# A recurrence kernel on one core: each power's transpose is squared beside the power instead of being turned from it

## The chip, the core and the metric

The kernel runs on one core of a Trainium2 chip. Its engines are TensorE (PE in the profile, PEld its weight loads), VectorE (DVE), ScalarE (ACT), GpSimd (POOL) and SyncE (SP, which here issues loads and stores). Each engine works through its own instructions in order; an instruction may wait for a semaphore that another engine raises, and what stands behind it on its engine waits too. Matmul results land in PSUM, where ACT and DVE read them. The metric is the time of one execution on the device, in microseconds; less is better.

## What is computed

The reference is one inference step of a two-layer trunk, on 128 context tokens and 512 latent tokens. Layer 0 mixes attention with a gated recurrence in two directions (cut to what matters here):

```
def _rwkv_step(S, xs):
    r, w, k, v, kk, a = xs
    sa = jnp.einsum('bhij,bhj->bhi', S, -kk)
    S = S * w[:, :, None, :] + sa[..., None] * (kk * a)[:, :, None, :] + v[..., None] * k[:, :, None, :]
    return S, jnp.einsum('bhij,bhj->bhi', S, r)
...
yf, sf = direction(wdf, adf, 0, s0f, False)
yb, sb = direction(wdb, adb, 1, s0b, True)
```

A scan over T tokens, forward and backward, for 8 heads with a state of 64x64 each. The rest of the program (attention, a gated feed-forward layer, a second layer with a mixture of experts) is not touched.

## The kernel before

The kernel does not walk token by token. It takes chunks of 128 tokens and, within a chunk, halves of 64 (HALVES, partitions 0 to 63 and 64 to 127). Inside a half the recurrence is a triangular system (I - A) u = rhs, with A strictly triangular, 64x64. Its inverse is the product of I + A^(2^l) for l = 0 to 5, so the kernel squares A five times (LEVELS = 5) and at each level multiplies the running inverse by the new power.

The function rwkv_stage has 20 **steps**: four pairs of heads (ct = 0 to 3) times five chunks (i = 0 to 4). In each step both directions (d = 0, 1), both heads of the pair (hh) and both halves (b) are done. The matrices of a step and where they lie:

- X holds the powers: X[b, slot, d, hh, 1, :] is the power, X[b, slot, d, hh, 0, :] its transpose; the two slots alternate by level. At level 0 the transpose is the masked product AM itself. The profile calls X a_power and AM a_masked.
- pU[d] is two PSUM banks for each direction (p_unit): bank 0 takes squares and turnings, bank 1 the products with the inverse. The inverse is TF (inverse_t).

A matmul takes a left operand that is already transposed, so squaring a power needs both the power and its transpose. Before the change a level goes like this, on PE and ACT by turns:

1. square_pe (L2318): four 64x64 products for each direction.
2. square_act (L2451): ACT copies the four results from PSUM to X as the new power.
3. power_turn_pe (L2327): PE multiplies the new power by the identity (K.ident), four products for each direction, which gives the transpose in PSUM.
4. power_turn_act (L2456): ACT copies it to X. The next level's squares wait for it.

inverse_pe (L2345) stands between the squares and the turnings on PE, for each direction, and inverse_dve (L2502) adds its result to TF. There are squares at levels 0 to 4, turnings at levels 0 to 3, inverses at levels 1 to 5.

The order is written out by hand, by the function walk, the same for each engine: for each step the levels 0 to 5, and at each level first level_pe (or ACT's, DVE's part), then one link of the **chain**, that is of the work of the step before with the state: chain_r (L2373, L2377) at level 0, which waits for state_mid from DVE (L2522), chain_u (L2387) at level 1, chain_a (L2396) at level 2, chain_u2 (L2405) at level 3, chain_end (L2416 to L2426) at level 5. Behind the chain stand the products of the next step: the builds (L2289) at levels 2 and 3, each followed by DVE's mask (L2491, 1.2 us), and the turning of the first power (L2300 to L2302) at level 4, with kb_act (L2435), a copy of 128x256, on ACT. Last in a level comes a piece of the preparation (PREP) of the next ct: products (L2092), ACT's square root (L2109), sigmoids (L2144) and exponentials, with loads of ACT's tables, DVE's reciprocals (L2119) and scans. It has fixed slots, in the first four steps of each ct but the last. All 20 steps are unrolled. During the recurrence there is no load but that of the masks.

Of the kernel before, what the change touches and what calls it, by code (L numbers as in the profile page):

```python
# [18 lines left out]
ACT = mybir.ActivationFunctionType  # L19
# [6 lines left out]
P = 128  # L26
# [4 lines left out]
HD = 64  # L31
# [1966 lines left out]
def rwkv_stage(K, zs, z, inputs, ring):  # L1998
# [12 lines left out]
    LEVELS = 5  # L2011
    NS = NT
    HALVES = (slice(0, HD), slice(HD, P))
    PIECES = ((0, 512), (512, T))
    R0, K0, V0, WD, AD, GD = 0, 4, 8, 12, 13, 14
    with ExitStack() as ctx:
# [10 lines left out]
        with ExitStack() as scan:  # L2027
# [12 lines left out]
            AM = K.sb(scan, "a_masked", [P, 3, 2, 2, 4 * P])  # L2040
            X = K.sb(scan, "a_power", [P, 2, 2, 2, 2, HD])
# [8 lines left out]
            pU = [K.ps(scan, f"p_unit{d}", [P, 2, 512]) for d in range(2)]  # L2050
# [6 lines left out]
            names = ("a", "xt", "x0", "kb", "tt0")  # L2057
            (u_m, u_xt, u_x0, u_kb, u_tt0) = (K.sig("un_" + n) for n in names)
            s_pairs = K.sig("rw_pairs")
            u_sq, u_xw, u_tq, u_tw, u_iv, u_tt = ([K.sig(f"un_{n}{d}") for d in range(2)] for n in  # L2060
                                                  ("squared", "power", "turning", "turned", "times", "inverse"))
            names = ("s", "r", "rb", "u", "ub", "r2", "rb2", "u2", "ub2", "y", "out")
            (c_s, c_r, c_rb, c_u, c_ub, c_r2, c_rb2, c_u2, c_ub2, c_y, c_out) = (K.sig("ch_" + n) for n in names)

# [196 lines left out]
            def unit(ct, i, d):  # L2261

                s = NS * ct + i
                return 2 * s + d, s, ORDER[d][i], s % 3
# [39 lines left out]
            def square_pe(pe, ct, i, d, l):  # L2304

                q, s, c, par = unit(ct, i, d)
                pA = pU[d][:, 0, :]
                if l == 0:
                    pe.wait_ge(u_x0.sem, u_x0.at(q + 1))
                    if s:  # L2310
                        pe.wait_ge(u_xw[d].sem, u_xw[d].at(LEVELS * s))
                else:
                    pe.wait_ge(u_xw[d].sem, u_xw[d].at(LEVELS * s + l))
                    pe.wait_ge(u_tw[d].sem, u_tw[d].at((LEVELS - 1) * s + l))
                for hh in range(2):
                    for b in HALVES:
                        xt = AM[b, par, d, hh, b] if l == 0 else X[b, l % 2, d, hh, 0, :]
                        mm = pe.matmul(pA[b, hh * HD:(hh + 1) * HD], xt, X[b, l % 2, d, hh, 1, :], start=True, stop=True)  # L2318
                mm.then_inc(u_sq[d].sem, 1)

            def power_turn_pe(pe, ct, i, d, l):

                q, s, c, par = unit(ct, i, d)
                pe.wait_ge(u_xw[d].sem, u_xw[d].at(LEVELS * s + l + 1))
                for hh in range(2):
                    for b in HALVES:
                        mm = pe.matmul(pU[d][b, 0, 2 * P + hh * HD:2 * P + (hh + 1) * HD], X[b, (l + 1) % 2, d, hh, 1, :], K.ident[b, b],  # L2327
                                       start=True, stop=True)
                mm.then_inc(u_tq[d].sem, 1)

            def inverse_pe(pe, ct, i, d, l):

# [15 lines left out]
            def level_pe(pe, ct, i, l):  # L2348
                if l < LEVELS:
                    for d in range(2):  # L2350
                        square_pe(pe, ct, i, d, l)
                for d in range(2):
                    if l:
                        inverse_pe(pe, ct, i, d, l)
                    if l < LEVELS - 1:
                        power_turn_pe(pe, ct, i, d, l)

            def values_of(ct, c, hh):
                return V[:, c, ct * P + hh * HD:ct * P + (hh + 1) * HD]
# [85 lines left out]
            def square_act(a, ct, i, d, l):  # L2445
                q, s, c, par = unit(ct, i, d)
                a.wait_ge(u_sq[d].sem, u_sq[d].at(LEVELS * s + l + 1))
                if l:

                    a.wait_ge(u_iv[d].sem, u_iv[d].at(LEVELS * s + l - 1))  # L2450
                a.activation(X[:, (l + 1) % 2, d, :, 1, :], pU[d][:, 0, 0:P].rearrange("p (h n) -> p h n", h=2), ACT.Copy).then_inc(u_xw[d].sem, 1)  # L2451

            def power_turn_act(a, ct, i, d, l):
                q, s, c, par = unit(ct, i, d)
                a.wait_ge(u_tq[d].sem, u_tq[d].at((LEVELS - 1) * s + l + 1))
                a.activation(X[:, (l + 1) % 2, d, :, 0, :], pU[d][:, 0, 2 * P:3 * P].rearrange("p (h n) -> p h n", h=2),  # L2456
                             ACT.Copy).then_inc(u_tw[d].sem, 1)

            def level_act(a, ct, i, l):
                if l < LEVELS:  # L2460
                    for d in range(2):
                        square_act(a, ct, i, d, l)
                if l < LEVELS - 1:
                    for d in range(2):
                        power_turn_act(a, ct, i, d, l)

            def ub_act(a, ct, i, d):
                q, s, c, par = unit(ct, i, d)
# [218 lines left out]
            steps = [(ct, i) for ct in range(CT) for i in range(NS)]  # L2687
# [85 lines left out]
            for d in range(2):  # L2773
                for sig in (u_sq[d], u_xw[d], u_iv[d], u_tt[d]):
                    sig.base += LEVELS * len(steps)
                for sig in (u_tq[d], u_tw[d]):
                    sig.base += (LEVELS - 1) * len(steps)


        with ExitStack() as last:  # L2780
# [866 lines left out]
```

## Time and profile before

| | us |
|---|---|
| median of 3 runs | 2760.75 (2757.59 to 2761.0) |
| profiled execution | 2765.16 |
| its span, first to last instruction | 2763.4 |
| busy PE / DVE / ACT / POOL | 2517.3 / 1610.5 / 1416.5 / 396.9 |
| the recurrence in it | 385.7 to 737.6, that is 351.9 |

The page cuts the span into 40 slices of 69 us. The recurrence fills slices 6 to 10. PEclk is the clock that TensorE was granted, in tenths of full speed.

```profile
PE   6998979999979999999799888896999999999993
DVE  3255555555464232312411488646888888888885
ACT  4235655554423333311322366525888888787883
PEclk9998979999999999999899899987999999999996
DMA  7630000000261222133165100318999999999994
```

In the timelines a row is a run of like instructions of one engine: its start, its length to the last one's end, the engine, the line, and in brackets how long the engine stood idle before it and who released it. Two of them overlap where one flows into the next; a matmul lasts some 0.2 us from start to result while the next starts much sooner. So for PE the starts are to be compared, not the lengths. Each 64x64 fp32 product stands as two records.

### The profile page before, as it was taken

The numbers are of one execution on the slowest core, as the hardware profiler recorded it, in microseconds if no ns is written. First come the engines' busy times: TensorE is split into PE (matmuls) and PEld (weight loads), VectorE is DVE, ScalarE is ACT, GpSimd is POOL, SyncE is SP. The second block draws the span as 40 slices with busy tenths as digits, with TensorE's granted clock in tenths as the row PEclk, the third lists the DMA queues.
The fourth block names the chain that finished last, engine by engine and source line by source line (L and its number), as shares of the span: only waits on it lengthen the run. The fifth ranks groups of instructions, "written<-read, shape, count | busy, mean of one in ns | idle before, by whom it ended". The sixth has DMA issues, their size and how long they took to land. (4 is left out here: it accounts for less than half of the span.)

```text
span 2763.4 us, 52457 instructions
## 1 busy us (share of the span) xinstructions
PE 2517.3 (91%) x19059; PEld 2185.6 (79%) x19059; DVE 1610.5 (58%) x2330; ACT 1416.5 (51%) x2277; POOL 396.9 (14%) x571
## 2 busy tenths in 40 slices
PE   6998979999979999999799888896999999999993
PEld 4887957777758888778677788786999999999992
DVE  3255555555464232312411488646888888888885
ACT  4235655554423333311322366525888888787883
POOL 1233122221113000001300243042000000000003
PEclk9998979999999999999899899987999999999996
DMA  7630000000261222133165100318999999999994
GB/s 267 206 118 6 14 5 3 3 3 3 82 236 46 77 75 76 34 118 114 46 226 180 39 16 15 107 50 284 380 385 381 383 384 377 385 377 384 376 382 189
DMA packets 262848, 472.26 MB, mean 171 GB/s; under 512 B 29436, under 2 KB 202108, under 8 KB 256548
## 3 DMA queue, kind: packets, MB, share of 16 engines
q1 hardware_dynamic: 255200, 445.69, 45.9%
q0 software_dynamic: 4416, 14.70, 1.4%
q10 hardware_dynamic: 3076, 9.71, 0.9%
q8 instruction: 109, 1.79, 0.3%
q14 instruction: 47, 0.39, 0.0%
HBM read 453.54 MB, written 16.48 MB: 170 GB/s over the span
## 5 line engine op out<-in xcount | busy, mean ns | idle before, releaser
L3399 DVE TENSOR_TENSOR m_lo<-m_raw,m_hi 128x1408 fp32r<-128x1408 f32 (+1 forms) x459 | 648.9, 1459 | 68.0 <-ACT m_hi L3258 65.5
L3258 ACT ACTIVATE m_hi<-m_raw 128x1408 fp32r<-128x1408 f32 (+1 forms) x459 | 549.5, 1247 | 45.5 <-DMA m_raw<-moe_w_gu 29.9
L213 PE MATMUL acc<-w_hi,h_hi 128*128 128x512 f32 (+1 forms) x1120 | 431.0, 385 | 18.1 <-PEq L2818 9.4
L195 DVE TENSOR_TENSOR w_lo<-w_raw,w_hi 128x1024 fp32r<-128x1024 f32 (+1 forms) x132 | 162.1, 1231 | 484.7 <-ACT w_hi L190 483.7
L215 PE MATMUL acc<-w_hi,h_lo 128*128 128x512 f32 (+1 forms) x1120 | 424.6, 379 | 0.0
L214 PE MATMUL acc<-w_lo,h_hi 128*128 128x512 f32 (+1 forms) x1120 | 424.2, 379 | 0.0
L190 ACT ACTIVATE w_hi<-w_raw 128x1024 fp32r<-128x1024 f32 (+1 forms) x134 | 135.3, 1015 | 460.5 <-PE acc L215 401.9
L213 PEld LDWEIGHTS acc<-w_hi,h_hi 128*128 128x128 f32 x1120 | 212.8, 190 | 79.2 <-issue 33.8
L215 PEld LDWEIGHTS acc<-w_hi,h_lo 128*128 128x128 f32 x1120 | 212.4, 190 | 34.0
L214 PEld LDWEIGHTS acc<-w_lo,h_hi 128*128 128x128 f32 x1120 | 212.9, 190 | 32.7
L3176 PE MATMUL p_gates<-m_hi,x_hi 128*128 128x352 f32 x544 | 181.5, 334 | 5.0 <-issue 5.0
L3177 PE MATMUL p_gates<-m_lo,x_hi 128*128 128x352 f32 x544 | 177.9, 327 | 0.0
L3179 PE MATMUL p_gates<-m_hi,x_lo 128*128 128x352 f32 x544 | 176.1, 324 | 0.0
L3179 PE MATMUL p_ups<-m_hi,x_lo 128*128 128x352 f32 x544 | 175.8, 323 | 0.0
L3176 PE MATMUL p_ups<-m_hi,x_hi 128*128 128x352 f32 x544 | 175.0, 322 | 0.0
L3177 PE MATMUL p_ups<-m_lo,x_hi 128*128 128x352 f32 x544 | 174.8, 321 | 0.0
L3192 PE MATMUL p_down<-m_hi,m_a_hi 128*128 128x512 f32 x374 | 150.3, 402 | 0.0
L3193 PE MATMUL p_down<-m_lo,m_a_hi 128*128 128x512 f32 x374 | 145.9, 390 | 0.0
L1230 POOL TENSOR_TENSOR x<-x,gated 128x512 f32<-128x512 f32 x30 | 47.0, 1584 | 533.2 <-DVE gated L1223 533.2
L3430 POOL DMA_INDIRECT x_gathered<-scratch_h_rows,slot_tokens x17 | 16.8, 988 | 739.6 <-PE p_turned L3145 732.1
L3196 PE MATMUL p_down<-m_hi,m_a_lo 128*128 128x512 f32 x374 | 115.8, 391 | 0.0
L3176 PEld LDWEIGHTS p_gates<-m_hi,x_hi 128*128 128x128 f32 x544 | 102.5, 189 | 6.1 <-issue 5.4
(408 smaller groups left out, 5018.2 us busy)
## 6 DMA issues: line engine op xcount, KB each, us to landing
m_raw<-moe_w_gu SPq DMA_DIRECT2D x544, 352.0 KB
m_raw<-moe_w_dn SPq DMA_DIRECT2D x187, 512.0 KB
ada_w<-ada_w SPq DMA_DIRECT2D x40, 1024.0 KB, 4.9
w_raw<-ffn_w_gu SPq DMA_DIRECT2D x88, 256.0 KB, 2.9
w_raw<-w_in_o SPq DMA_DIRECT2D x24, 512.0 KB, 5.8
w_raw<-ffn_w_dn SPq DMA_DIRECT2D x22, 512.0 KB, 3.8
w_raw<-w_in_e SPq DMA_DIRECT2D x28, 384.0 KB, 4.9
scratch_y_slots<-y_slot ACTq DMA_DIRECT2D x18, 512.0 KB, 6.3
```

What stands on the lines that cost most here:

```text
L190: eng.activation(hi, self.raw_of(c, k), ACT.Copy).then_inc(self.hi.sem, 1)
L195: eng.tensor_tensor(lo, self.raw_of(c, k), hi, ALU.subtract).then_inc(self.lo.sem, 1)
L213: eng.matmul(out, hi, whi[:, b, :], start=first, stop=False)
L214: eng.matmul(out, hi, wlo[:, b, :], start=False, stop=False)
L215: mm = eng.matmul(out, lo, whi[:, b, :], start=False, stop=last)
L3176: pe.matmul(acc[:, c % 2, 0:ECH], xh[:, j, :], h[:, b, half, :], start=start, stop=False)
L3177: pe.matmul(acc[:, c % 2, 0:ECH], xh[:, j, :], l[:, b, half, :], start=False, stop=False)
L3179: mm = pe.matmul(acc[:, c % 2, 0:ECH], xl[:, j, :], h[:, b, half, :], start=False, stop=stop)
L3192: pe.matmul(pD[:, half, :], ah[:, k, :], whi[:, s, cs], start=k == 0, stop=False)
L3193: pe.matmul(pD[:, half, :], ah[:, k, :], wlo[:, s, cs], start=False, stop=False)
L3258: a.activation(whi[:, u % MSPLIT, 0:size(u)], raw[:, s, 0:size(u)], ACT.Copy).then_inc(s_hi.sem, 1)
L3399: dve.tensor_tensor(wlo[:, u % MSPLIT, 0:n], raw[:, u % MRAW, 0:n], whi[:, u % MSPLIT, 0:n], ALU.subtract).then_inc(s_lo.sem, 1)
```

## The change

The turnings (power_turn_pe, power_turn_act) are gone. square_pe now makes two products where it made one: form 1, lhs = transpose, rhs = power, gives the squared power as before; form 0, with the two operands exchanged, gives its transpose. The four results of one half, two heads by two forms, lie side by side in bank 0 of pU[d], in X's own order. ACT copies them in one operation of 128x256. At level 4 the transpose is not needed, and only form 1 is done. The squares no longer wait for the turned copy (u_tw), and two pairs of semaphores are gone.

```diff
-                    pe.wait_ge(u_tw[d].sem, u_tw[d].at((LEVELS - 1) * s + l))
                 for hh in range(2):
-                    for b in HALVES:
-                        xt = AM[b, par, d, hh, b] if l == 0 else X[b, l % 2, d, hh, 0, :]
-                        mm = pe.matmul(pA[b, hh * HD:(hh + 1) * HD], xt, X[b, l % 2, d, hh, 1, :], start=True, stop=True)
+                    for form in ((0, 1) if l < LEVELS - 1 else (1,)):
+                        for b in HALVES:
+                            xt, x = (AM[b, par, d, hh, b] if l == 0 else X[b, l % 2, d, hh, 0, :]), X[b, l % 2, d, hh, 1, :]
+                            at = (2 * hh + form) * HD
+                            mm = pe.matmul(pA[b, at:at + HD], *((xt, x) if form else (x, xt)), start=True, stop=True)
                 mm.then_inc(u_sq[d].sem, 1)
-
-            def power_turn_pe(pe, ct, i, d, l):
...
                     if l:
                         inverse_pe(pe, ct, i, d, l)
-                    if l < LEVELS - 1:
-                        power_turn_pe(pe, ct, i, d, l)
...
-                a.activation(X[:, (l + 1) % 2, d, :, 1, :], pU[d][:, 0, 0:P].rearrange("p (h n) -> p h n", h=2), ACT.Copy).then_inc(u_xw[d].sem, 1)
-
-            def power_turn_act(a, ct, i, d, l):
...
+                forms = slice(0, 2) if l < LEVELS - 1 else slice(1, 2)
+                a.activation(X[:, (l + 1) % 2, d, :, forms, :], pU[d][:, 0, 0:2 * P].rearrange("p (h f n) -> p h f n", h=2, f=2)[:, :, forms, :],
+                             ACT.Copy).then_inc(u_xw[d].sem, 1)
```

PE's instructions at the second step of the program, a step that begins with a table load: the squares of level 0 and what follows. p_unit_94 and p_unit_95 are pU of direction 0 and 1, p_chain is the chain's. Before:

```order
L2318 MATMUL p_unit_94<-a_power,a_masked 64x64 x4
L2318 MATMUL p_unit_95<-a_power,a_masked 64x64 x4
L2327 MATMUL p_unit_94<-ident,a_power 64x64 x4
L2327 MATMUL p_unit_95<-ident,a_power 64x64 x4
L2373 MATMUL p_chain<-v_rows,a_masked 64x64 x4
L2377 MATMUL p_chain<-state_mid,zr_68 64x128 x2
L2373 MATMUL p_chain<-v_rows,a_masked 64x64 x4
L2377 MATMUL p_chain<-state_mid,zr_69 64x128 x2
L2318 MATMUL p_unit_94<-a_power 64x64 x4
L2318 MATMUL p_unit_95<-a_power 64x64 x4
L2345 MATMUL p_unit_94<-inverse_t,a_power 64x64 x4
L2327 MATMUL p_unit_94<-ident,a_power 64x64 x4
```

The same place in the changed kernel, from the squares of direction 1 on (those of direction 0 stand ahead of them in the same form):

```order
L2319 MATMUL p_unit_95<-a_masked,a_power 64x64 x2
L2319 MATMUL p_unit_95<-a_power,a_masked 64x64 x2
L2319 MATMUL p_unit_95<-a_masked,a_power 64x64 x2
L2319 MATMUL p_unit_95<-a_power,a_masked 64x64 x2
L2362 MATMUL p_chain<-v_rows,a_masked 64x64 x4
L2366 MATMUL p_chain<-state_mid,zr_68 64x128 x2
L2362 MATMUL p_chain<-v_rows,a_masked 64x64 x4
L2366 MATMUL p_chain<-state_mid,zr_69 64x128 x2
L2319 MATMUL p_unit_94<-a_power 64x64 x8
L2319 MATMUL p_unit_95<-a_power 64x64 x8
L2336 MATMUL p_unit_94<-inverse_t,a_power 64x64 x4
L2336 MATMUL p_unit_95<-inverse_t,a_power 64x64 x4
```

The chain stands directly behind the squares of level 0, and the two inverses directly behind those of level 1; the turnings between them are gone. On ACT, at the same place, before (the table load for the sigmoids, the copies of levels 0 and 1, and the chain's u):

```order
L2144 ACT_TABLE_LOAD
L2144 ACTIVATE log_decay<-p_build,channel_vectors 128x512
L2144 ACTIVATE log_decay<-p_build,channel_vectors 128x128
L2451 ACTIVATE a_power<-p_unit_94 128x2x64
L2451 ACTIVATE a_power<-p_unit_95 128x2x64
L2456 ACTIVATE a_power<-p_unit_94 128x2x64
L2456 ACTIVATE a_power<-p_unit_95 128x2x64
L2451 ACTIVATE a_power<-p_unit_94 128x2x64
L2451 ACTIVATE a_power<-p_unit_95 128x2x64
L2456 ACTIVATE a_power<-p_unit_94 128x2x64
L2456 ACTIVATE a_power<-p_unit_95 128x2x64
L2474 ACTIVATE u<-p_chain 64x128 x2
```

And in the changed kernel:

```order
L2144 ACT_TABLE_LOAD
L2144 ACTIVATE log_decay<-p_build,channel_vectors 128x512
L2144 ACTIVATE log_decay<-p_build,channel_vectors 128x128
L2441 ACTIVATE a_power<-p_unit_94 128x256
L2441 ACTIVATE a_power<-p_unit_95 128x256
L2441 ACTIVATE a_power<-p_unit_94 128x256
L2441 ACTIVATE a_power<-p_unit_95 128x256
L2456 ACTIVATE u<-p_chain 64x128 x2
```

Eight copies of 128x2x64 became four of 128x256; the table load and the sigmoids keep their place ahead of them. DVE's, POOL's and SP's instructions are the same as before.

## Rows read from the trace of the kernel before

**Rows 1.** Busy time by stretch: us, busy of each engine (instructions), PEclk, DMA share, GB/s.
```profile
385.70:737.60 351.90, 328.02 (x6772) 270.24 (x6772) 191.32 (x490) 182.66 (x590) 70.82 (x106) 0.96 0.01 3
538.80:542.20 3.40, 3.40 (x56) 3.07 (x56) 0.73 (x3) 0.79 (x3) 0.00 (x0) 0.50 0.02 5
```
**Rows 2.** Waits of the recurrence, 385.7 to 737.6 us: total us, times, longest.
```profile
PEld p_unit L2327 <- ACT a_power L2451: 22.6, 42, 1.9
```
**Rows 3.** Groups by line and shape, 385 to 738 us: busy us, mean ns, idle before.
```profile
L2327 PE MATMUL p_unit<-ident,a_power 64*64 64x64 f32 x1280 | 66.4, 229 | 16.7 <-ACT a_power L2451 13.5
...
L2318 PE MATMUL p_unit<-a_power 64*64 64x64 f32 x1280 | 60.2, 233 | 0.1
...
L2451 ACT ACTIVATE a_power<-p_unit 128x128 f32<-128x128 f32 x200 | 49.1, 278 | 76.5 <-PE p_unit L2318 75.0
...
L2435 ACT ACTIVATE kb_rows<-p_build 128x256 f32<-128x256 f32 x40 | 13.1, 386 | 0.0
...
L2144 ACT ACT_TABLE_LOAD x6 | 7.7, 1283 | 14.5 <-PE p_build L2092 14.5
```
**Rows 4.** Timeline of an undisturbed step, levels 0 to 2: start us, length us, work [idle before].
```profile
679.02 0.68 PE L2318 MATMUL p_unit<-a_power,a_masked 64*64 64x64 f32 x16
...
679.52 0.51 ACT L2451 ACTIVATE a_power<-p_unit 128x128 f32<-128x128 f32 x2 [1.66 <-PE p_unit L2318]
...
679.85 0.68 PE L2327 MATMUL p_unit<-ident,a_power 64*64 64x64 f32 x16
...
681.51 0.68 PE L2318 MATMUL p_unit<-a_power 64*64 64x64 f32 x16
...
682.03 0.40 PE L2345 MATMUL p_unit<-inverse_t,a_power 64*64 64x64 f32 x8
...
682.34 0.45 PE L2327 MATMUL p_unit<-ident,a_power 64*64 64x64 f32 x8
...
682.86 0.40 PE L2327 MATMUL p_unit<-ident,a_power 64*64 64x64 f32 x8
...
683.32 0.85 PE L2318 MATMUL p_unit<-a_power 64*64 64x64 f32 x16
...
683.98 0.43 PE L2345 MATMUL p_unit<-inverse_t,a_power 64*64 64x64 f32 x8
...
684.44 0.45 PE L2327 MATMUL p_unit<-ident,a_power 64*64 64x64 f32 x8
```
**Rows 5.** Timeline of a step that begins with a table load, levels 0 and 1.
```profile
535.56 1.28 ACT L2144 ACT_TABLE_LOAD   x1 [2.80 <-PE p_build L2092]
535.62 0.55 PEld L2318 LDWEIGHTS p_unit<-a_power,a_masked 64*64 64x64 f32 x16
...
537.69 0.45 ACT L2451 ACTIVATE a_power<-p_unit 128x128 f32<-128x128 f32 x2
...
538.02 0.68 PE L2327 MATMUL p_unit<-ident,a_power 64*64 64x64 f32 x16 [1.71 <-ACT a_power L2451]
...
540.46 1.12 PE L2318 MATMUL p_unit<-a_power 64*64 64x64 f32 x16
...
542.68 0.45 PE L2387 MATMUL p_chain<-rhs,inverse_t 64*64 64x64 f32 x8
...
544.33 0.54 PEld L2318 LDWEIGHTS p_unit<-a_power 64*64 64x64 f32 x16
```
**Rows 6.** Timeline of the step at 479 us: squares of levels 1 to 3, and DVE.
```profile
481.08 0.68 PE L2318 MATMUL p_unit<-a_power 64*64 64x64 f32 x16
...
484.91 0.68 PE L2318 MATMUL p_unit<-a_power 64*64 64x64 f32 x16
...
488.72 0.68 PE L2318 MATMUL p_unit<-a_power 64*64 64x64 f32 x16
...
489.98 1.74 DVE L2119 RECIPROCAL L_before<-log_decay 128x256 f32<-128x256 f32 x1
```
**Rows 7.** Timeline of the step at 518.3 us: the chain's first product of level 0.
```profile
519.94 0.31 PEld L2373 LDWEIGHTS p_chain<-v_rows,a_masked 128*64 128x64 f32 x8 [0.28 <-DVE state_mid L2522]
```

More of the change, by code:

```diff
@@ L2059, in rwkv_stage @@
             s_pairs = K.sig("rw_pairs")
-            u_sq, u_xw, u_tq, u_tw, u_iv, u_tt = ([K.sig(f"un_{n}{d}") for d in range(2)] for n in
-                                                  ("squared", "power", "turning", "turned", "times", "inverse"))
+            u_sq, u_xw, u_iv, u_tt = ([K.sig(f"un_{n}{d}") for d in range(2)] for n in
+                                                  ("squared", "power", "times", "inverse"))
             names = ("s", "r", "rb", "u", "ub", "r2", "rb2", "u2", "ub2", "y", "out")
@@ L2313, in square_pe @@
                     pe.wait_ge(u_xw[d].sem, u_xw[d].at(LEVELS * s + l))
-                    pe.wait_ge(u_tw[d].sem, u_tw[d].at((LEVELS - 1) * s + l))
                 for hh in range(2):
-                    for b in HALVES:
-                        xt = AM[b, par, d, hh, b] if l == 0 else X[b, l % 2, d, hh, 0, :]
-                        mm = pe.matmul(pA[b, hh * HD:(hh + 1) * HD], xt, X[b, l % 2, d, hh, 1, :], start=True, stop=True)
-                mm.then_inc(u_sq[d].sem, 1)
-            def power_turn_pe(pe, ct, i, d, l):
[L2323 to L2329, printed above, removed]
+                    for form in ((0, 1) if l < LEVELS - 1 else (1,)):
[3 more added lines that the diff above has]
+                            mm = pe.matmul(pA[b, at:at + HD], *((xt, x) if form else (x, xt)), start=True, stop=True)
+                mm.then_inc(u_sq[d].sem, 1)
             def inverse_pe(pe, ct, i, d, l):
@@ L2450, in square_act @@
                     a.wait_ge(u_iv[d].sem, u_iv[d].at(LEVELS * s + l - 1))
-                a.activation(X[:, (l + 1) % 2, d, :, 1, :], pU[d][:, 0, 0:P].rearrange("p (h n) -> p h n", h=2), ACT.Copy).then_inc(u_xw[d].sem, 1)
-            def power_turn_act(a, ct, i, d, l):
[L2454 to L2457, printed above, removed]
+                forms = slice(0, 2) if l < LEVELS - 1 else slice(1, 2)
+                a.activation(X[:, (l + 1) % 2, d, :, forms, :], pU[d][:, 0, 0:2 * P].rearrange("p (h f n) -> p h f n", h=2, f=2)[:, :, forms, :],
+                             ACT.Copy).then_inc(u_xw[d].sem, 1)
             def level_act(a, ct, i, l):
@@ L2462, in level_act @@
                         square_act(a, ct, i, d, l)
-                if l < LEVELS - 1:
-                    for d in range(2):
-                        power_turn_act(a, ct, i, d, l)
             def ub_act(a, ct, i, d):
@@ L2775, in rwkv_stage @@
                     sig.base += LEVELS * len(steps)
-                for sig in (u_tq[d], u_tw[d]):
-                    sig.base += (LEVELS - 1) * len(steps)
         with ExitStack() as last:
```

## The prediction, made before the changed kernel was run

> **What bounds the kernel now.** I read first the busy times of the stretch that the edit touches: the recurrence runs from 385.7 to 737.6 us, 351.9 us in which PE is busy 328.0, DVE 191.3 and ACT 182.7, at a mean granted clock of 0.96, with the DMA engines idle [rows 1]. Nothing is loaded in it, and everything after it starts when it ends, so a microsecond won here is a microsecond of the kernel. PE is the bound, but not an unbroken one. The waits say what breaks it: LDWEIGHTS of the turned power (L2327) stood 22.6 us over 42 times for ACT's copy of the power (L2451) [rows 2]. Then the timelines: of an undisturbed step (679 us) [rows 4], of one where ACT is late (535.6 us) [rows 5], of one with the square roots in it [rows 6], and one piece where DVE is late [rows 7].
>
> The unit of the sum comes from [rows 4]: four 64x64 products (eight matmul records) take g = 0.235 us of PE's queue, whichever they are: turned power of direction 1 and the two chain products, 682.86 to 683.32, are two such groups in 0.46. Sixteen records and the switch to the inverse take 0.52 (681.51 to 682.03). A group's result reaches ACT 0.50 after its start (679.02 to 679.52).
>
> **The change part by part.**
>
> Matmuls. The 640 turning products (1280 records of L2327) go, and 640 squaring products come. A record of the one is 229 ns, of the other 233 [rows 3], and each product is two records in both, so PE's work is unchanged: 0 us.
> The Trainium skill (TensorE: Matmul & The Clock Gate, Terms) speaks against the change here: its transpose mode is four times faster for fp32, so a turning would be much cheaper than a product. The rows of L2327 and L2318 do not show it, as said; what it would make of the time is the third rival.
>
> ACT. Two copies of 128x128 at 278 ns (200 at L2451, 160 more of the same kind at L2456) become one of 128x256 on four levels of five. The kb_rows copy has that shape: 386 ns [rows 3]. ACT does 160 x (0.278 + 0.278 - 0.386) = 27 us less, beside PE's work: 0 us by itself. What it alters is latency: the copy of one direction is ready 0.50 + 0.39 + 0.05 = 0.94 us after the last square of it is issued as a group of four; with eight in a row, 1.17 after the level's start for direction 0, and some 1.6 for direction 1.
>
> Waits. Before, each level made PE wait inside itself: squares, ACT, turning, ACT, next squares. After, PE issues squares (4g = 0.94, and 0.05 for the switch), inverses (2g = 0.47) and chain work before it needs the copies again: 1.46 us at the least, against 1.17. Direction 1 is needed 0.47 later still, at 1.93, and there at 1.6. So in an undisturbed level there is no wait left. What goes, by level, in [rows 4]:
> Level 0: squares to turning 0.83 where the squares take 2g = 0.47: **0.36**. The level becomes 0.94 + (681.51 - 679.85 - 0.47) = 2.13, before 2.49.
> Level 1: inverse to turning 0.31 for 0.235, and turning to turning 0.52 for 0.47: **0.12**; the level becomes 1.69, before 1.81.
> Level 2: squares to inverse 0.66 for 0.52, inverse to turning 0.46 for 0.235, and as at level 1 some 0.05: **0.42**. Level 3 has the same 0.1 as level 1. Level 4 has no turning and keeps its length; its end waits for DVE's masks, whose start is set by the build of level 3, and that moves with the rest.
> Sum: **1.0 us** for an undisturbed step. Five steps are such (the last ct, in which nothing is prepared for a next one): **5.0 us**.
>
> Late ACT [rows 5]. Six steps begin with a table load for the sigmoids (L2144, six loads of 1283 ns [rows 3]). Before: squares at 535.62, ACT free at 537.69, turning at 538.02, then the chain, and the next squares only at 540.46: 4.84 us. After, the turned power is behind PE already and the chain (L2373, L2377) needs no copy of ACT, so it runs in the shadow of the table load; PE is done with level 0 at +2.13 and waits for a copy that begins at +2.07 and lasts 0.39: next squares at +2.51. **2.3 us** saved.
> At level 1 of these steps (540.46 to 544.33, 3.87 us) PE runs at half clock: 0.50 from 538.8 to 542.2 [rows 1], after the 1.7 us in which it did nothing. With 0.4 of idling left I take the clock to hold. The level then needs 0.99 for its squares, 0.47 for the inverses, and 1.65 for L2387 and the sigmoids' products behind it (542.68 to 544.33, at full clock): 3.11. **0.76 us** saved. Levels 2 and 3 give 0.35 and 0.1. Together 3.5 us, in six steps: **21.0 us**.
>
> Square roots [rows 6]. Two steps like the one at 479 us: level 0 gives 0.35; level 1, 481.08 to 484.91, has products of the same sizes behind L2387 and becomes 3.1 too, 0.7 less; level 2, 484.91 to 488.72, loses its wait for ACT's square roots, since the copy is now wanted 2.7 us after the squares and no longer 0.75: 2.69 for 3.81, 1.1 less. But the reciprocal of 1.74 us that DVE starts at 489.98 is fixed to the masks, and level 3 has grown shorter, so the next masks come later against it: 0.1 lost. 2.1 us each, **4.1 us**. The first step of all, at half clock throughout and without a chain: I take **1.5**.
>
> Late DVE [rows 7]. In six steps (two for each ct but the last) the chain at level 0 waited for DVE's state_mid; it still does, so level 0 gives nothing. Three of them keep 0.6 us and three 0.5 (in these the second build waits for DVE's tilde at level 3): **3.3 us**.
>
> The sum is 5.0 + 21.0 + 4.1 + 1.5 + 3.3 = **35 us**. The profiled execution took 2765.2 (span 2763.4), the median of the runs shown is 2760.75, 0.16% less; the saving is taken from the median: **2726 us**.
>
> Bounds. The 128x256 copy from PSUM is shown, contiguous in both views as here. Not shown is the row of eight squares without a turning between: at best as now, and at worst each level keeps 0.1 us more, 80 levels, 8 us. Not shown either is the clock after a wait of 0.4: if it falls, see below. In the other direction the first step and the stages behind, whose half-clock stretches shift, may give up to 6 us more.
>
> **The rivals.**
> (1) The half clock comes all the same, in six places. A stretch of 3.4 us holds 1.7 us of full-speed work less; against it stands that gaps of 0.3 (679.85) go unpunished. 6 x 1.6 = 10 us back: 2736.
> (2) The wait only moves: the next squares wait as long for the larger copies as the turning did. For it: ACT is what PE stood for. Against it: the cover of 1.46 us against 1.17. It would need copies a further 0.3 us late, then 0.44 more, on every level; time 2755 to 2760, within 0.2%.
> (3) Turning was cheap and the products are dear. If PE gave 3/4 of g more to each of 160 turnings, 160 x 0.18 = 28 us, the gain shrinks to 7: 2754. The two means of [rows 3] speak against it.
> (4) Slower: the pairing of the halves is lost. A group of four takes 0.235 since partitions 0 to 63 and 64 to 127 run beside each other, b being the innermost loop. In the new row of eight a tile of X is the weight in one product and the moving operand in the next. If this made neighbours wait, a product would cost 0.117 for 0.059, on 1440 squaring products: 84 us, and the result 49 us slower, 2810. It decides from 0.024 us a product (35 / 1440). The inverse, whose operands differ again, has the same g, so I give it little. The Trainium skill (TensorE: Matmul & The Clock Gate, The mechanism) lets a weight load overlap matmuls only where the row group differs; b still alternates, so by that rule the pairing holds, and in [rows 4] it does.
> That the change doesn't do what it says is hardly open: the products and copies are in the listing of instructions as the diff has them.
>
> **How the numbers follow.** The forecast has 0.74; (1) 0.14; (2) 0.05; (3) 0.03; (4) 0.04. The forecast alone spans 2718 to 2736 by the bounds, and (1) with some of the 0.1 a level takes it to 2744; from 2717 to 2744 I leave out less than 2 in 10. Differences under 0.2% (5.5 us) can't be told from none. Faster: 0.74 + 0.14 + 0.03 = 0.91; same: 0.05; slower: 0.04.
>
> **What would show it.** The time from the squares of level 0 to those of level 1 in a late-ACT step falls from 4.84 to 2.5, and in an undisturbed step from 2.49 to 2.13; an undisturbed step lasts 14.9 for 15.9 us. No half clock between 405 and 737 us. The recurrence ends 35 us sooner and the stages behind are as long as before. I am wrong if groups of eight squares start more than 0.47 us apart, if PE's waits for ACT's copy reappear at the squares with 20 us or so, or if a stage behind gives time back.

## The result, and the profile after

The changed kernel takes **2723.19 us** (median of 4 runs, 2719.23 to 2725.91), the one before 2760.88 in 4 runs beside it: a ratio of 0.9863, with a 95% interval of 0.9845 to 0.988. That is 37.7 us less; 2726, 35 less, was forecast. Its profiled execution took 2721.46, span 2719.4.

The change also ran later beside other kernels (label e11_after_again). There the kernel before had a median of 2756.68, and the changed one 2721.46: 35.2 us less, 0.9869 (0.9854 to 0.9884), where 37 was expected. The forecast of 35 lies just below both. The recurrence in its trace is as in the first to 0.3 us.

> The changed kernel once more, beside the two others on one chip, as the measure for them and for what the stages behind the recurrence do from one execution to the next: 37 us faster than before; in its trace the recurrence as in the first one to 0.5 us, and the stages behind it free to differ by 3 us.

Busy times, from the page of the changed kernel:

```profile
PE 2486.5 (91%) x19059; PEld 2166.9 (80%) x19059; DVE 1607.8 (59%) x2330; ACT 1391.2 (51%) x2117; POOL 395.6 (15%) x571
```

ACT has 25 us less to do (27 forecast). Busy time by stretch (us, then busy of PE, PEld, DVE, ACT, POOL with instructions, PEclk, DMA share, GB/s):

```profile
405.00:734.00 329.00, 307.98 (x6572) 251.72 (x6567) 205.72 (x501) 159.60 (x419) 75.44 (x108) 1.00 0.09 33
386.30:395.00 8.70, 8.41 (x174) 6.78 (x170) 3.47 (x6) 6.00 (x13) 0.89 (x2) 1.00 0.01 4
```

The recurrence ends at some 705 us now. Between 405 and 734 us the clock is full throughout; the 0.50 of [rows 1] is gone in all six places. The second row is the first step, to which I come back.

The waits of the recurrence (us, times, longest), 385 to 703 us, in the changed kernel:

```profile
ACT a_power L2441 <- PE p_unit L2319: 84.8, 65, 2.3
PEld p_build L2300 <- DVE a_masked L2473: 9.6, 19, 0.8
PEld p_chain L2362 <- DVE state_mid L2504: 3.8, 6, 0.6
PEld p_unit L2319 <- ACT a_power L2441: 3.2, 6, 0.5
```

PE stood 22.6 us over 42 times for ACT's copies [rows 2]; it now stands for them six times, 3.2 us in all. Nothing has come in their place that is as long: PE's largest wait is now that for DVE's masks at the turning of the first power (L2300), 9.6 us over 19 times, which was 7.9 before. ACT waits for PE, as it did. The same stretch by line and shape (busy us, mean ns, idle before):

```profile
L2319 PE MATMUL p_unit<-a_power 64*64 64x64 f32 x2240 | 82.6, 221 | 1.8 <-ACT a_power L2441 1.8
...
L2441 ACT ACTIVATE a_power<-p_unit 128x256 f32<-128x256 f32 x160 | 60.0, 383 | 76.2 <-PE p_unit L2319 71.1
```

The squares are no dearer in their new row of eight, 221 ns against 233 [rows 3], and the large copy has the length of the one it was priced by, 383 for 386.

An undisturbed step (start us, length us, work, idle before), to be laid beside [rows 4]:

```profile
677.14 1.15 PE L2319 MATMUL p_unit<-a_power 64*64 64x64 f32 x32
678.12 0.63 PE L2336 MATMUL p_unit<-inverse_t,a_power 64*64 64x64 f32 x16
...
678.59 0.45 PE L2376 MATMUL p_chain<-rhs,inverse_t 64*64 64x64 f32 x8
...
678.82 1.15 PE L2319 MATMUL p_unit<-a_power 64*64 64x64 f32 x32
...
681.50 1.15 PE L2319 MATMUL p_unit<-a_power 64*64 64x64 f32 x32
...
684.39 0.68 PE L2319 MATMUL p_unit<-a_power 64*64 64x64 f32 x16
```

Squares of level 1 start at 677.14, of level 2 at 678.82, of level 3 at 681.50, of level 4 at 684.39, and no other engine stops PE between them. The squares of level 1 end their row at 678.12 (0.98), the inverses take 0.47, the chain's products 0.23.

A step that begins with a table load, to be laid beside [rows 5]:

```profile
516.76 1.28 ACT L2144 ACT_TABLE_LOAD   x1 [2.81 <-PE p_build L2092]
516.83 0.33 PE L2319 MATMUL p_unit<-a_masked,a_power 64*64 64x64 f32 x4
...
517.91 0.45 PE L2362 MATMUL p_chain<-v_rows,a_masked 128*64 128x64 f32 x8
...
518.89 0.66 ACT L2441 ACTIVATE a_power<-p_unit 128x256 f32<-128x256 f32 x2
...
519.33 1.15 PE L2319 MATMUL p_unit<-a_power 64*64 64x64 f32 x32 [0.29 <-ACT a_power L2441]
...
522.43 1.15 PE L2319 MATMUL p_unit<-a_power 64*64 64x64 f32 x32
```

Before, PE stood 1.71 us behind the squares; now it goes on to the chain (L2362) while ACT loads its table, and stands 0.29 for the copy at 518.89. Level 0 lasts 519.33 - 516.83 = 2.50, level 1 3.10.

All levels, from the start of one's squares to the next's, levels 0 to 4, before and after:

| steps | before | after | saved each |
|---|---|---|---|
| undisturbed, 5 (lengths of the middle three) | 2.49, 1.81, 3.10, 3.02, 5.43 | 2.13, 1.68, 2.68, 2.90, 5.43 | 1.03 |
| ACT late, 6 | 8.70 for the first two, 3.03, 3.02, 5.43 | 2.50, 3.10, 2.68, 2.90, 5.67 | 3.33 |
| square roots, 2 | 19.09 in all | 1.69, 3.10, 2.81, 2.90, 6.49 | 2.1 |
| DVE late, 3 and 3 | 17.33 and 15.76 in all | 16.66 and 15.21 | 0.67 and 0.55 |
| first | 19.74 | 15.95 | 3.8 |

Sum: 5.2 + 20.0 + 4.2 + 3.7 + 3.8 = 36.9 us. From the first squares to the last product of the chain the two profiles differ by 36.8, and by 37.1 with the repeat. The two spans differ by 44.0, more than the medians: the profiled execution before lay 4.3 above its median, that of the changed kernel 1.7 below. In the traces the rest comes in behind the recurrence, some 3 us each between 744 and 760 us and at 1860 to 1960 us; the second of these differences stands in the profiles of the experiments too, also where they gain little, so it belongs to that one execution of before.

### The profile page after: what moved, and what is told of

It reads as the page before. It is cut to its first block and busy times, and to the rows that moved or that the text cites. A ratio compares the mean times of both kernels' runs of the same rounds, so it can differ in the third digit from the quotient of the medians.

```text
span 2719.4 us, 52138 instructions
## 1 busy us (share of the span) xinstructions
PE 2486.5 (91%) x19059; PEld 2166.9 (80%) x19059; DVE 1607.8 (59%) x2330; ACT 1391.2 (51%) x2117; POOL 395.6 (15%) x571
## 5 line engine op out<-in xcount | busy, mean ns | idle before, releaser
L214 PEld LDWEIGHTS acc<-w_lo,h_hi 128*128 128x128 f32 x1120 | 213.3, 190 | 32.6
L2441 ACT ACTIVATE a_power<-p_unit 128x256 f32<-128x256 f32 (+1 forms) x200 | 69.6, 361 | 89.9 <-PE p_unit L2319 84.8
```

Of the source, the lines that this page charges most:

```text
L214: eng.matmul(out, hi, wlo[:, b, :], start=False, stop=False)
```

## The experiments

All times are medians, each with those of the kernel before on the same chip. Levels are measured as in the table above. In diffs the lines of the kernel before, or of the changed one, are marked -.

**The change at level 0 alone (e1_level0), and at levels 1 to 3 alone (e2_levels123).** The theory has the gain where a copy of a busy ACT stood between squares and chain, at level 0. The rival has it in the number of ACT's copies, which is three times larger on three levels. The edit on the kernel before, for the first; the second has (1, 2, 3):

```
+            DOUBLED = (0,)
...
+                    for form in ((0, 1) if l in DOUBLED else (1,)):
...
-                    if l < LEVELS - 1:
+                    if l in TURNED:
                         power_turn_pe(pe, ct, i, d, l)
```

> The kernel before with the change at level 0 of each step alone; levels 1 to 3 still turn the copied power. My theory (what is won is PE's waits inside a level): late-ACT steps win 2.33 us at level 0 and 0.6 at level 1, because the clock holds (6 x 2.93 = 17.6); the undisturbed steps 0.36 (5 x 0.36 = 1.8), the two steps with square roots 0.35, the first step 0.6: 20 to 21 us faster than before. Rival (what counts is that ACT has fewer copies): 40 of the 160 copies go, a quarter of the 38 us, some 9 us.

> The kernel before with the change at levels 1 to 3 alone; level 0 still turns. My theory: the half clock after the table load stays. 5 x 0.64 for undisturbed steps, 6 x 0.6 in late-ACT steps, 2 x 1.7 in the steps with square roots, 6 x 0.55 in the steps where DVE is late, 0.9 in the first: 14 us faster than before. Rival (fewer copies): three quarters of the 38 us, 28 us.

Measured: e1_level0 2734.88 against 2758.22 (0.9914, 0.9897 to 0.993), 23.3 us less; e2_levels123 2739.83 (0.9931, 0.9914 to 0.9947), 18.4 less. In the first, level 0 of the late-ACT steps takes 2.50 as in the whole change, and the clock is full in all of them:

```profile
405.30:710.00 304.70, 290.70 (x6318) 240.91 (x6312) 179.24 (x463) 162.71 (x511) 68.96 (x102) 1.00 0.01 3
```

In the second, PE still stands 1.71 us for the copy behind the table load in all six late-ACT steps, and in four of them it falls to half clock. In the worst two level 0 takes 5.34 and level 1 4.54 us. Two stretches by engine, and PE's timeline in the second:

```profile
492.30:499.00 6.70, 6.21 (x97) 5.64 (x97) 1.98 (x6) 1.93 (x8) 0.00 (x0) 0.50 0.01 2
440.00:447.00 7.00, 5.29 (x119) 4.25 (x114) 2.65 (x9) 4.28 (x12) 0.00 (x0) 1.00 0.01 4
```
```profile
441.84 0.68 PE L2333 MATMUL p_unit<-ident,a_power 64*64 64x64 f32 x16 [1.71 <-ACT a_power L2460]
```

The stretch from 440 us and its stand-still at 441.84 show the other case: after the same stand-still the clock stayed full, in two places of the six (level 0 4.06 us, level 1 3.10). Half clock lasts 6.8 us in two places and 3.4 in two, and the six late-ACT steps together are 2.4 us shorter than before, not the 3.6 of the expectation.

By the medians alone the two experiments can hardly be told apart, since their intervals overlap; by the traces (below) level 0 carries the larger part. Three of four turnings are gone in e2_levels123, and what they give is the small terms of [rows 4] (levels of 1.68, 2.68 and 2.90). Counted in the profiles from the same matmul at some 360 us to the first squares of the last step, the recurrence is 21.5 us shorter in e1_level0 (20 to 21 expected) and 14.3 in e2_levels123 (14 expected), together 35.8, where the whole change gives 37.0 by the same count. What the medians give beyond that, 1.8 and 4.1 us, lies outside the recurrence and was not followed. The rival by the number of copies wanted 28 for the second and 9 for the first, and falls.

**Two copies for one (e3_two_copies).** The changed kernel, with the large copy done as two of 128x128:

```
-                a.activation(X[:, (l + 1) % 2, d, :, forms, :], ...
+                for f in ((0, 1) if l < LEVELS - 1 else (1,)):
+                    copied = a.activation(X[:, (l + 1) % 2, d, :, f, :], ...
```

> The changed kernel, but ACT copies the squared powers and the transposes by two operations of 128x128 instead of one of 128x256; PE's work and its order are those of the changed kernel. My theory: the copies are off the path; the second one ends 0.45 us after the first begins, not 0.39, so the next squares could start at 1.23 us of a level and start at 1.46 or later; only the six late-ACT steps pay, 0.1 us each: within 2 us of the changed kernel, 36 us faster than before. Rival (fewer copies are what counts): most of the gain is gone, 10 us faster than before.

Measured: 2721.87 against 2758.22 (0.9867, 0.9851 to 0.9884), 36.4 us less, as for the changed kernel. ACT has its copies back,

```profile
L2441 ACT ACTIVATE a_power<-p_unit 128x128 f32<-128x128 f32 x360 | 79.0, 277 | 83.9 <-PE p_unit L2319 82.4
```

79.0 us of them for 60.0 of the large and some 11 of the level-4 ones (40 at 0.28), and the kernel is no slower; level 0 of the late steps is 2.56 for 2.50. That one operation copies both gives next to nothing here. What is left as the cause is that PE makes the transpose without waiting for the copied power.

**Copy work doubled (e6_copy_twice).** Each large copy is done once more into unused columns of its PSUM bank, ahead of itself:

```
+                if l < LEVELS - 1:
+                    a.activation(pU[d][:, 0, 2 * P:4 * P], pU[d][:, 0, 0:2 * P], ACT.Copy)
```

> The changed kernel, in which ACT copies each pair of squared power and transpose twice, first into an unused part of the same PSUM bank: 160 more operations of 128x256, each of 0.38 us, 0.26 where they follow each other. My theory: the copies have room. At level 1 direction 0's is ready at 1.43 us of the level and wanted at 1.68, direction 1's at 1.95 and wanted at 2.15; only the late-ACT steps pay, 0.3 us each at level 0: 2 us slower than the changed kernel. Rival (ACT's load is on the path): 160 x 0.26, some 40 us slower, the whole gain gone.

Measured: 2726.34 against 2758.92 (0.9888, 0.9873 to 0.9903), 32.6 us less, so 60 us more work on ACT (160 copies of 0.38) cost some 3 to 5, where 2 were expected. The medians alone would hardly carry so small a difference; the levels show where it lies. In the steps they cost where ACT was already late, with the square roots too, which was not expected: late-ACT level 0 2.80 for 2.50, its level 1 3.21 for 3.10, level 2 with the square roots 3.64 for 2.81; 6 x 0.41 + 2 x 0.83 = 4.1. The first step is another 1 us longer (17.06 for 15.95 and 16.18). An undisturbed step keeps 2.13, 1.68, 2.68, 2.90. The wait in a late step:

```profile
520.50 1.26 PE L2319 MATMUL p_unit<-a_power 64*64 64x64 f32 x32 [0.59 <-ACT a_power L2443]
```

This is the test of the second rival, that the squares would wait as the turnings had: even with a copy later by 0.3 us at each level, there was cover left.

**Idle products in the place of the wait (e5_filled, e9_filled_half).** Does the half clock come from PE's stand-still of 1.71 us [rows 5]? The kernel before, with products of the identity with itself behind the squares of level 0 in the six late-ACT steps, 26 pairs of halves in the first and 13 in the second:

```
+                if l == 0 and ct < CT - 1 and i in (1, 3):
+                    pe.wait_ge(u_tt[1].sem, u_tt[1].at(LEVELS * (NS * ct + i)))
+                    for n in range(FILL):
+                        for b in HALVES:
+                            pe.matmul(pU[1][b, 1, 2 * P:2 * P + HD], K.ident[b, b], K.ident[b, b], start=True, stop=True)
```

> The kernel before, with 26 pairs of 64x64 products of the identity, whose results nobody reads, put behind the squares of level 0 in the six late-ACT steps; PE works through them for 1.5 us while it would otherwise stand and wait for ACT's copy. Nothing else changes. My theory (the half clock at levels 0 and 1 is the price of that wait): no half clock in the recurrence, level 0 of these steps 4.05 us for 4.84, level 1 3.22 for 3.87: 6 x 1.4, 8 to 9 us faster than before, though PE does more. Rival (the clock falls for another cause): no faster than before, up to 1 us slower.

> As the run with 26 pairs of idle products, but 13 pairs, since the 26 took PE 3.0 us and not the 1.5 that I had reckoned, and so lengthened level 0 from 4.84 to 5.17 us. 13 pairs take 1.5 us and end when ACT's copy comes. If the half clock is the price of the wait: none in the recurrence, level 0 of the six late-ACT steps 4.05 us, level 1 3.22, together 1.4 less than the 8.70 before: 8 to 9 us faster than before. Rival (the clock falls for another cause, or a shorter filling doesn't hold it): 0 to 3 us faster.

Measured: e5_filled 2756.63 against 2758.92 (0.9993, 0.9984 to 1.0002), not to be told from no change where 8 to 9 us were expected. The filling was priced wrongly:

```profile
533.16 3.20 PE L2358 MATMUL p_unit<-ident 64*64 64x64 f32 x104
536.20 0.63 PE L2327 MATMUL p_unit<-ident,a_power 64*64 64x64 f32 x16
```

26 pairs are 104 records, and at 29 ns each they filled 3.0 us, not the 1.5 of the wait. Level 0 became 5.17 for 4.84, and level 1 3.22 for 3.87: the clock held, and the filling ate what that gave. With half of it:

```profile
532.17 1.68 PE L2358 MATMUL p_unit<-ident 64*64 64x64 f32 x52
534.05 0.68 PE L2327 MATMUL p_unit<-ident,a_power 64*64 64x64 f32 x16 [0.19 <-ACT a_power L2458]
...
535.71 0.68 PE L2318 MATMUL p_unit<-a_power 64*64 64x64 f32 x16
```

The squares are issued at 531.66, the copy comes when it came, and the next squares start at 535.71: level 0 4.06, level 1 3.22, 7.28 for 8.70. The kernel takes 2749.22 against 2756.68 (0.9973, 0.9962 to 0.9983), 7.5 us less, where 8 to 9 were expected, and the levels say 6 x 1.42 = 8.5. Nothing but 52 idle records in each late-ACT step was added. So the half clock is a price of the stand-still: it came after all six of before, and after none of the twelve that were filled. It is not a fixed price: e2_levels123 has the same stand-still of 1.71 us six times and paid in four of them only, up to 2.7 us (9.88 for levels 0 and 1, against 7.16). What decides between these cases was not found. In the kernel before it was 1.42 us a time, and of the 20.0 us that the late-ACT steps gave, 8.5 are clock.

**The pairing of the halves taken apart (e4_half_outer).** The slower rival rested on products of partitions 0 to 63 and 64 to 127 running beside each other. In the changed kernel the half becomes the outer loop:

```
-                for hh in range(2):
-                    for form in ((0, 1) if l < LEVELS - 1 else (1,)):
-                        for b in HALVES:
+                for b in HALVES:
+                    for hh in range(2):
+                        for form in ((0, 1) if l < LEVELS - 1 else (1,)):
```

> The changed kernel with the squares of partitions 0 to 63 all issued ahead of those of 64 to 127, where they alternated. It prices the rival in which the halves lose their pairing. If a product takes 0.117 us alone and 0.059 in a pair: of eight products in a row only one overlaps, 0.82 to 0.94 us for 0.47, in 160 groups, and 0.1 more in the 40 groups of level 4: 60 to 75 us slower than the changed kernel, about 2790 us. If the order does not matter to PE: the time of the changed kernel.

Measured: 2746.33 against 2758.22 (0.9953, 0.9934 to 0.9971): 24 us slower than e3_two_copies beside it, which runs as the changed kernel does, not 60 to 75. Pieces of PE's timeline, level 0, and the change from level 1 to 2:

```profile
676.96 0.32 PE L2319 MATMUL p_unit<-a_masked,a_power 64*64 64x64 f32 x2
677.13 0.28 PE L2319 MATMUL p_unit<-a_power,a_masked 64*64 64x64 f32 x2
677.24 0.33 PE L2319 MATMUL p_unit<-a_masked,a_power 64*64 64x64 f32 x4
677.36 0.33 PE L2319 MATMUL p_unit<-a_power,a_masked 64*64 64x64 f32 x4
677.53 0.33 PE L2319 MATMUL p_unit<-a_masked,a_power 64*64 64x64 f32 x4
...
678.11 0.28 PE L2319 MATMUL p_unit<-a_masked,a_power 64*64 64x64 f32 x2
678.22 0.28 PE L2319 MATMUL p_unit<-a_power,a_masked 64*64 64x64 f32 x2
678.43 0.45 PE L2362 MATMUL p_chain<-v_rows,a_masked 128*64 128x64 f32 x8
```
```profile
680.80 0.22 PE L2336 MATMUL p_unit<-inverse_t,a_power 64*64 64x64 f32 x1
680.80 0.22 PE L2319 MATMUL p_unit<-a_power 64*64 64x64 f32 x1
```

At both ends of level 0 only one half has work, and two records take 0.11 us (677.13 to 677.24, 678.11 to 678.22): unpaired, a record costs twice what it costs in pairs, as was priced. But between them eight records take 0.29 us (677.24 to 677.53), though the program lists eight of one half ahead of eight of the other. A trace does not name the half; read from the starts, the second half begins when the first has done four records, and they go on side by side. The halves are two streams, each in its own order, and one runs ahead of the other by four records, 0.28 us; even the inverses (L2336) of one half run beside the squares of the other (680.80), which the program lists before them. What this costs shows where both halves have to meet: before chain_r (L2362), whose products read all 128 partitions, and before the builds (L2289), which write all of them. Level 0 takes 2.52 for 2.13: four records at either end are on their own, 0.23 more, and the 24 between at 0.036 us each instead of 0.029, 0.16. Level 3 takes 3.29 for 2.90, and levels 1 and 2 together, which have one meeting point, 4.92 for 4.36. So a record outside a pair does cost double, but the order of listing leaves most of the pairs whole: 0.4 to 0.6 us for each meeting point, 20 us in all (by the count from 360 us the recurrence is 17.2 us shorter than before, where the changed kernel's is 37.0).

**What stands in the way next (e7_end4, e8_end4_later, e10_state5).** Three edits on the changed kernel, each with those before it: the last link of the chain at level 4 for 5, where it covers PE's wait for the masks; ACT's sigmoids for direction 0 one slot later, behind the copies; and DVE's state_mid computed at the end of a step for the next:

```
-                         {0: (chain_r,), 1: (chain_u,), 2: (chain_a,), 3: (chain_u2,), 5: (chain_end,)})
+                         {0: (chain_r,), 1: (chain_u,), 2: (chain_a,), 3: (chain_u2,), 4: (chain_end,)})
```
```
-                PREP += [(at, "pe", lora_pe(d, 0)), (at, "act", lora_act(d, 0)),
+                PREP += [(at, "pe", lora_pe(d, 0)), (at + 1, "act", lora_act(d, 0)),
```
```
+                        if l == LEVELS:
+                            for d in range(2):
+                                state_dve(dve, ct, i, d)
...
-                    walk(dve, "dve", first_dve, masks_dve, (), level, {0: (state_dve, rb_dve), 2: (rb2_dve,), 5: (end_dve,)})
+                    walk(dve, "dve", first_dve, masks_dve, (), level, {0: (rb_dve,), 2: (rb2_dve,), 4: (end_dve,)})
```

> The changed kernel with chain_end (PE) and its end_dve (DVE) moved from level 5 to level 4, ahead of the turning that waits for DVE's second mask. chain_end is 1.93 us of PE's work whose inputs are there. My theory: PE's wait of 0.27 us (0.5 in the steps with square roots) for that mask goes, 19 times; the first power, whose copy chain_end used to hide, is still ready, since the last inverses stand between: 5 to 6 us faster than the changed kernel. Rival: the wait moves to the end of level 5 (inverse_t from DVE, or the first power from ACT): the same time or up to 5 us slower.

> As the one before, and ACT's table load and first sigmoids (L2144) stand one slot later, behind the copies of level 0 instead of ahead of them. My theory: PE's wait of 0.37 us before level 1 in the six late-ACT steps goes, and the sigmoids' results are just there when PE's products of level 1 want them: 2 us faster than the one before. Rival: the copies of level 1 are late instead: no gain.

> As the kernel with chain_end at level 4 and the sigmoids one slot later, and DVE makes the next state_mid at the end of level 5, ahead of the piece of preparation there, instead of at level 0 behind it. My theory: PE's wait for state_mid at level 0 of the six late-DVE steps (level 0 lasts 3.27 us there, 2.08 elsewhere) goes: 5 to 7 us faster than that kernel, 14 to 16 us faster than the changed kernel. Rival: DVE's preparation, pushed back by 0.6 us, delays the builds of the next ct: no gain.

Measured: e7_end4 2719.70 (0.9861, 0.9846 to 0.9876) and e8_end4_later 2716.43 (0.9855, 0.984 to 0.987), both against 2758.92; e10_state5 2709.31 against 2756.68 (0.9829, 0.9815 to 0.9842), 12.2 us below the changed kernel on the same chip, where 14 to 16 were expected. By the medians the first two cannot be told from the changed kernel, since the intervals overlap; what is said of them here rests on the levels. The third can: its slowest run took 2714.4, the fastest of the changed kernel beside it 2720.8.

The first gave about half of the 5 to 6 us expected, 3.3 by the steps. Level 4 fell from 5.43 to 5.01 as it should, but in the late-DVE steps level 0 rose from 2.70 to 3.27: the products of chain_r came sooner, and DVE's state_mid did not. The second took level 0 of the late-ACT steps to 2.13, a level without any wait, 6 x 0.37 = 2.2 us, where 2 were expected; the medians say 3.3. In it the new bound is seen plainly, PE standing for state_mid behind a DVE operation of the preparation:

```profile
497.29 0.82 DVE L2233 TENSOR_TENSOR kt<-kd,L 128x640 f32<-128x640 f32 x1 [0.57 <-ACT L L2215]
...
498.03 0.61 DVE L2504 SCALAR_TENSOR_TENSOR state_mid<-state_sum,masks,head_ones 128x128 f32<-128x128 f32 x2
498.43 0.45 PE L2362 MATMUL p_chain<-v_rows,a_masked 128*64 128x64 f32 x8 [1.12 <-DVE state_mid L2504]
```

The third moves state_mid ahead of that operation, and the wait is gone:

```profile
493.70 0.61 DVE L2504 SCALAR_TENSOR_TENSOR state_mid<-state_sum,masks,head_ones 128x128 f32<-128x128 f32 x2
494.35 0.82 DVE L2233 TENSOR_TENSOR kt<-kd,L 128x640 f32<-128x640 f32 x1
```
```profile
494.81 0.40 PE L2362 MATMUL p_chain<-v_rows,a_masked 128*64 128x64 f32 x8
```

Level 0 is 2.13 there too, for 3.27: 6 x 1.14 = 6.8 us. This version, 2709.3 us, beats both kernels.

## Why the prediction was right, point by point

- **What bounds the kernel.** PE is the bound, and what could be won from it was its wait for a copy, not an amount of work. Three experiments bear this out: as many copies as before cost nothing (e3_two_copies), 60 us more of ACT's time cost 4 (e6_copy_twice), and one level of four, the one with the long wait in it, brought 23.3 us (e1_level0). Not tried was the kernel before with nothing but the chain's products put between squares and turnings at level 0; it would cover the same wait, and how much of the gain needs the second product of each pair stays open.
- **Matmuls at 0 us.** Right: PE has as many records as before, and a squaring record is 221 ns where a turning one was 229 [rows 3]. The third rival (a turning is cheap) is refuted: an undisturbed level 0 is as short as equal prices make it. What the Trainium skill (TensorE: Matmul & The Clock Gate, Terms) says of transpose mode does not reach these products with the identity, which run as ordinary ones.
- **An undisturbed step, 1.0 us, five times.** Right within 0.03: 2.13, 1.68, 2.68 and 2.90 measured for 2.13, 1.69, 2.69 and 2.93, 14.82 for 14.9. The reason was the cover, 1.46 us of other products against 1.17 of latency, and e6_copy_twice shows it to hold even 0.3 us later.
- **Late ACT, 3.5 us, six times.** 2.50 and 3.10 for 2.51 and 3.11. The half clock stayed away, so the first rival did not come. That it is the stand-still that brings it was an assumption; e9_filled_half shows that it does not come without one, and e2_levels123 that it need not come with one. The term came out as 3.33, since level 4 grew by 0.24. The step that missed it was "level 4 keeps its length". In a timeline of the changed kernel, and then of the same place in the kernel before:

```profile
525.83 1.54 POOL L2166 TENSOR_TENSOR iclr<-iclr,kk 128x640 f32<-128x640 f32 x1
...
526.37 1.69 DVE L2176 TENSOR_TENSOR L_before<-half_end,L 128x640 f32<-128x640 f32 x1
...
529.64 0.45 PE L2300 MATMUL p_build<-ident,a_masked 64*64 64x64 f32 x8 [0.49 <-DVE a_masked L2473]
```
```profile
547.72 1.54 POOL L2166 TENSOR_TENSOR iclr<-iclr,kk 128x640 f32<-128x640 f32 x1
...
548.62 1.33 DVE L2176 TENSOR_TENSOR L_before<-half_end,L 128x640 f32<-128x640 f32 x1
...
551.78 0.45 PE L2300 MATMUL p_build<-ident,a_masked 64*64 64x64 f32 x8 [0.25 <-DVE a_masked L2491]
```

DVE's centring of the preparation (L2176, in the other three of the six steps L2174) ends 0.69 us behind POOL's product L2166 in both kernels: 525.83 + 1.54 to 528.06, and 547.72 + 1.54 to 549.95. The distance is the same in all six steps, so it is POOL's work that fixes its end. In the changed kernel DVE reaches it sooner and so spends 1.69 us on it for 1.33. With levels 2 and 3 shorter, the inverse and the mask queue up behind it, and PE, at the turning of the first power, waits 0.49 us for the mask, where it waited 0.25. I had seen this for the reciprocals in the square-root steps, where 0.1 was set aside, and not for this one. e1_level0, whose levels 2 and 3 are as before, keeps 5.43; e2_levels123 has the 5.67.
- **Square roots, 2.1 us, twice.** Right: 16.99 for 19.09, with level 2 at 2.81 where 2.69 was reckoned.
- **Late DVE, 3.3 us.** Measured 3.7, from 0.67 and 0.55 for 0.6 and 0.5. The chain still waits for state_mid six times, 3.8 us in the waits above.
- **First step, 1.5 us.** Mis-sized: 3.8 (3.6 in the repeat). "At half clock throughout" was the step that failed. Before, half clock lasts far into it; a stretch of the kernel before, to be laid beside 386.30 to 395.00 of the changed one above:

```profile
386.50:395.40 8.90, 8.43 (x104) 6.52 (x102) 0.57 (x2) 6.34 (x17) 0.00 (x0) 0.50 0.01 2
```

Here 104 records run at 0.50, there 174 at 1.00. After the change the clock came back at 386.3 (387.1 in the repeat), in e1_level0 at 388.4 and in e2_levels123 near 390, against 395.4 before and 393.3 and 395.7 in e5_filled and e9_filled_half, whose first step is as before. Counted from the first squares, it is back after 9.4 to 9.6 us where the first step is as before, after 5.8 in e2_levels123, 2.6 in e1_level0 and 2.7 in e3_two_copies, and after 1.4 and 2.9 in the two profiles of the changed kernel. With fewer stops of PE it came sooner, though one kernel scatters by 1.5 us. Which of the stops decides was not tried.
- **The fourth rival.** Its mechanism, lost pairing, did not occur: 32 records of squares took 0.98 us (677.14 to 678.12), in pairs as before. What a loss of all pairs by the operands would cost (84 us by the text) was not measured. e4_half_outer shows that the order of listing does not bring it: 60 to 75 us were expected there and some 20 came, since the pairing had been taken as one group's own matter.
- **Stages behind as long as before.** Not shown wrong, and only roughly confirmed: from the end of the recurrence to the last matmul the first profile is 5.4 us shorter than that of before, the repeat 0.4 us longer.

The near hit of the sum has luck in it: 1.0 us too much for the late-ACT steps, 2.3 too little for the first, 0.4 too little for late DVE and 0.3 for the rest leave only 2 us of the 36.9. The span given for the forecast alone, 2718 to 2736, is 2 us wider on either side than its own bounds of 6 and 8 us make it; nothing rests on that.

## What to carry to other kernels

Where a result goes through a second engine and back several times in a row, count the trips and not the operations: here as much PE work and nearly as much ACT work were kept, and a trip fewer at each level let other products of PE cover the one that was left. Price a wait with what follows it: PE's stand-still of 1.7 us cost another 1.4 through the clock in the kernel before, so a gap on a bound engine is worth looking at in the granted clock behind it. And when levels get shorter, look for the long operations of other engines that lie at fixed places (here one of 1.54 us on POOL, behind which one of DVE ends), for these are what is late next.

## What the runs showed of the hardware that was not expected

- Products of 64x64 on the lower and on the upper half of the partitions form two streams, of which one can run ahead of the other into the next group of instructions, here by four records (e4_half_outer; read from the starts). A record of one half takes some 57 ns of the queue alone and 29 in pairs. Listing them in groups of eight a half costs 0.4 to 0.6 us for each place where a product on all 128 partitions follows.
- PE fell to half clock after standing 1.71 us behind 0.5 us of squares, and kept the full clock in the same place when 1.7 us of idle products filled it (e9_filled_half). In e2_levels123 it stood 1.71 us in six places and kept the full clock in two of them. A wait of 0.29 in the changed kernel, of 0.59 in e6_copy_twice and of 1.12 in e8_end4_later left it at full clock each time.
- A DVE operation on 128x640 (L2174, L2176) that began while POOL worked on its product of 128x640 (L2166) ended 0.69 us after POOL's: it took 1.33 us where it began 0.65 before POOL's end (the kernel before), and 1.69 where it began 1.00 before it (the changed one).
